# A two-layer decoder trunk on 8 cores: loads and rotary tables of the opening in another order, the first tile's attention moved into it, and steps re-ordered at the joints between tiles, before the MLP and at the final norms

## The chip, the cores and the metric

The kernel runs on all 8 cores of one Trainium2 chip, each core on its own data, without communication. The metric is the device time in microseconds (us) of the slowest core.

## The reference

```python
def reference(x, mem, positions, ...):          # x (4, 4096, 1024), mem (4, 256, 1024)
    for l in range(2):
        h = rmsnorm(x, norm_mix_g[l])
        gb, gc, xc, q, k, v = jnp.split(h @ w_in[l], splits, axis=-1)   # 512,512,512,512,128,128
        conv_out = gb * causal_short_conv(gc * xc, conv_w[l])           # depthwise, width 3
        q, k = apply_rotary(q, cos, sin), apply_rotary(k, cos, sin)
        attn_out = sliding_window_attention(q, k, v, sinks[l])          # 8 heads, 2 kv heads, window 128
        x = x + concat(rmsnorm(conv_out), rmsnorm(attn_out)) @ w_out[l]
        x = x + memory_cross_attention(rmsnorm(x), rmsnorm(mem), wx_q[l], wx_kv[l], wx_o[l])
        x = x + square(relu(rmsnorm(x) @ w_up[l])) @ w_down[l]          # 1024 -> 4096 -> 1024
    return rmsnorm(x, final_g)
```

## The kernel before

A core holds 2048 tokens and a halo of 256 before them (T = 2304), channels on partitions, f32, in SBUF all the time (`xT`). Weights come from HBM as f32 and are cast to bf16 by the transfer into a ring (`Wr`). Matmuls are bf16 with 128x128 weights.

Each layer has three stages. **p1** walks the tiles of `tiles1`. In layer 0 these are tile 0 (128 tokens, keys, values and convolution state only), tile 1 (128 tokens, the "short tile") and tiles 2 to 9 of 256 tokens; in layer 1 a halo tile and 8 full ones. For a tile: norm (`norm_a` the squares on ScalarE, `norm_r` their sum on VectorE, `norm_b` the product with ones on TensorE, a Ln and an Exp on ScalarE and eight scaled copies on VectorE, `x_h`), keys and values (`kv_a`, rotary in `kv_b`), queries (`q_a`, `q_b`), convolution (`conv_a` three projections, `conv_b` products with diagonal matrices `dg`), attention for each block of 128 (`att_s` scores, exponent and mask, `att_pv` sums and values), group norms (`g_sq`, `g_red`, `g_rest`; which 0 is convolution, 1 attention) and the output projection `p1_proj`. Iteration i works on the attention of tile i, projects tile i-1, projects queries, keys, values and convolution of tile i+1 (`nx`) and norms tile i+2 or i+3. The keys and values of the 256 memory tokens are made on the way (`mem_sq`, `mem_norm` whose scaling runs on GpSimd, `mem_piece` 0 to 7). **p2** is the cross-attention by tiles; it also norms halves of the MLP's input (`a_sq`, `a_red`, `a_rest`; the one in flight is finished by `a_pend`). **p3** is the MLP in steps (e, i) of a weight piece e and a token tile i: `up` of the next step, then `down` of this one, each output chunk `oc` added to `xT`. In the last layer it also does the final norms (`fin`), of which the second half of a tile waits in the list `rest`, and the output transfers.

All work is written out in one order by hand. Each engine runs its instructions in that order and waits on semaphores that a tracker (`Trk`) puts in front of an instruction. TensorE fills eight PSUM banks, taken in the order of least recent use. `begin` is the opening of layer 0: the rotary tables (`rope_split`, `rope_angles`, `rope_table`, `rope_spread`), the norms of tiles 0 to 3, and their keys, values and convolutions. The queue of a load is that of the engine named: `tk.dma("pool", ...)`, `load_w` and `xload` without a queue go through GpSimd's queue, in order, "sp" through SyncE's. `after("sp", ("x", 0, 16))` holds SyncE until tokens 1024 to 1279 have landed.

The order of the loads is this:

```python
tk.dma("pool", mski[:], masks_d[:], dsem("ldm"), W=["mski"])
load_kv(0); load_cv(0, 0); xload(256, 512); load_cv(0, 1); xload(512, 768)
load_q(0); load_wout(0); xload(768, 1024); xload(1024, 1280)
```

(`xload(0, 256)` stands ahead of them, on the same queue.)

## Time and profile before

| | us |
|---|---|
| median of 3 runs | 1883.87 |
| the runs | 1865.79, 1883.87, 1945.28 |
| the profiled execution, its own time | 1865.94 |
| its span on the slowest core (core 4), first to last instruction | 1864.9 |
| spans of the 8 cores | 1857.8 to 1864.9 |

The span is what the trace covers; 1.0 us of the profiled execution's own time lies around it. Granted TensorE clocks of the cores are 0.979 to 0.987 of full speed.

### The profile page before, as it was taken

The numbers are of one execution on the slowest core, as the hardware profiler recorded it, in microseconds if no ns is written. First come the engines' busy times: TensorE is split into PE (matmuls) and PEld (weight loads), VectorE is DVE, ScalarE is ACT, GpSimd is POOL, SyncE is SP. The second block draws the span as 40 slices with busy tenths as digits, with TensorE's granted clock in tenths as the row PEclk, the third lists the DMA queues.
The fourth block names the chain that finished last, engine by engine and source line by source line (L and its number), as shares of the span: only waits on it lengthen the run. The fifth ranks groups of instructions, "written<-read, shape, count | busy, mean of one in ns | idle before, by whom it ended". The sixth has DMA issues, their size and how long they took to land.

```text
span 1864.9 us, 33585 instructions; the slowest of 8 cores (1857.8 to 1864.9 us)
## 1 busy us (share of the span) xinstructions
PE 1765.1 (95%) x12355; PEld 1164.5 (62%) x12413; DVE 1185.1 (64%) x2406; ACT 704.5 (38%) x1244; POOL 71.2 (4%) x99
## 2 busy tenths in 40 slices
PE   3789998999999999999999999999999999999996
PEld 2667786888755555555557778678884444444444
DVE  4578776667575555555577878675766455455677
ACT  4445555556431111111125555564662111111232
POOL 1002000000000000000000200000000000000000
PEclk7889999999999999999999999999999999999998
DMA  9700203600332221111311011252024122200022
GB/s 183 209 1 13 35 13 61 121 2 1 61 59 41 46 46 23 24 35 34 69 24 24 13 24 24 41 97 47 1 47 86 28 46 46 40 6 1 23 68 91
DMA packets 23911, 86.38 MB, mean 46 GB/s; under 512 B 2116, under 2 KB 11332, under 8 KB 17096
## 3 DMA queue, kind: packets, MB, share of 16 engines
q0 software_dynamic: 11296, 69.47, 20.1%
q1 hardware_dynamic: 12456, 14.76, 2.4%
q8 instruction: 103, 1.69, 0.4%
q14 instruction: 56, 0.46, 0.1%
HBM read 140.06 MB, written 8.39 MB: 80 GB/s over the span
## 4 chain that ended last, share of the span: by engine, by line
PE 86%; DVE 8%; issue 3%; ACT 3%; DMA 0%; DVEq 0%; ACTq 0%; POOLq 0%
PE ps L168 85%; PE ps L180 1%; DVE S L484 1%; DVE S L760 1%; DVE xT_sb L1171 1%; DVE xT_sb L1151 1%; DVE S L474 1%; DVE S L751 1%; DVE S L627 1%; DMA xT_sb<-xT 0%; ACT S L461 0%; ACT S L463 0%; ACT S L622 0%; DVE S L641 0%; DVE H L484 0%
## 5 line engine op out<-in xcount | busy, mean ns | idle before, releaser
L168 PE MATMUL ps<-S,Wr 128*128 128x256 bf16 (+4 forms) x9494 | 1464.9, 314 | 17.9 <-DVE S L484 8.2
L168 PEld LDWEIGHTS ps<-S,Wr 128*128 128x128 bf16 x9536 | 919.2, 98 | 541.1 <-issue 34.6
L1136 ACT ACTIVATE S<-ps 128x448 bf16<-128x448 f32 (+2 forms) x292 | 162.2, 556 | 681.7 <-PE ps L168 681.7
L1151 DVE TENSOR_TENSOR xT_sb<-ps,xT_sb 128x448 f32<-128x448 f32 (+3 forms) x592 | 365.5, 631 | 57.3 <-PE ps L168 30.9
L1138 DVE TENSOR_TENSOR S<-S 128x448 bf16<-128x448 bf16 (+2 forms) x292 | 116.1, 399 | 323.7 <-ACT S L1136 323.6
L168 PE MATMUL ps<-H,Wr 128*128 128x256 bf16 (+2 forms) x1496 | 178.0, 277 | 8.2 <-DVE H L484 7.9
L168 PEld LDWEIGHTS ps<-H,Wr 128*128 128x128 bf16 x1496 | 144.6, 102 | 33.9 <-issue 15.3
L484 DVE SCALAR_TENSOR_TENSOR S<-xT_sb,cst_sb,S 128x256 bf16<-128x256 f32 (+2 forms) x360 | 140.1, 461 | 37.6 <-ACT S L463 37.6
L468 ACT ACTIVATE S<-xT_sb 128x2048 bf16<-128x2048 f32 (+3 forms) x62 | 110.8, 1788 | 9.9 <-DVE xT_sb L1151 9.9
L503 DVE TENSOR_TENSOR xT_sb<-ps,xT_sb 128x512 f32<-128x512 f32 (+1 forms) x136 | 86.1, 668 | 43.0 <-PE ps L168 42.7
L461 ACT ACTIVATE S<-ps,cst_sb 128x256 f32<-128x256 f32 (+2 forms) x97 | 45.1, 465 | 99.8 <-PE ps L168 93.6
L702 ACT ACTIVATE S<-ps 128x512 bf16<-128x512 f32 x132 | 75.0, 594 | 13.8 <-PE ps L168 7.5
L1015 DVE TENSOR_TENSOR S<-ps,S 128x512 bf16<-128x512 f32 (+1 forms) x68 | 44.6, 672 | 45.5 <-ACT S L1009 40.8
L760 DVE SCALAR_TENSOR_TENSOR S<-S,cst_sb 128x256 bf16<-128x256 f32 (+1 forms) x136 | 56.3, 476 | 26.2 <-ACT S L463 26.2
L474 DVE TENSOR_TENSOR S<-S 128x1024 bf16<-128x1024 bf16 (+2 forms) x112 | 60.2, 537 | 11.6 <-ACT S L468 5.7
L998 ACT ACTIVATE S<-ps 128x512 bf16<-128x512 f32 (+1 forms) x68 | 37.2, 573 | 61.7 <-PE ps L168 61.7
L706 DVE TENSOR_TENSOR S<-S,mski 128x1024 bf16<-128x1024 bf16 x66 | 44.9, 689 | 14.1 <-ACT S L702 13.4
L733 ACT ACTIVATE S<-S 128x512 f32<-128x512 f32 x33 | 20.8, 630 | 81.1 <-DVE S L726 75.4
L989 ACT CAST H<-ps 128x512 bf16<-128x512 f32 (+1 forms) x68 | 38.6, 569 | 31.4 <-PE ps L168 30.7
L168 PE MATMUL ps<-S,ones_d 128*128 128x256 bf16 (+2 forms) x200 | 34.4, 278 | 16.5 <-ACT S L468 16.5
L463 ACT ACTIVATE S<-S 128x256 f32<-128x256 f32 (+2 forms) x97 | 39.4, 407 | 8.9
L622 ACT COPY S<-ps 128x512 f32<-128x512 f32 (+1 forms) x34 | 19.4, 572 | 61.7 <-PE ps L168 55.4
(93 smaller groups left out, 839.3 us busy)
## 6 DMA issues: line engine op xcount, KB each, us to landing
Wr<-w_up POOLq DMA_DIRECT2D x16, 1024.0 KB, 8.6
Wr<-w_down POOLq DMA_DIRECT2D x16, 1024.0 KB, 8.7
Wr<-wx_kv POOLq DMA_DIRECT2D x16, 512.0 KB, 5.2
outT<-xT_sb SPq DMA_DIRECT2D x28, 256.0 KB, 2.5
Wr<-w_cv POOLq DMA_DIRECT2D x4, 1536.0 KB, 15.9
xT_sb<-xT POOLq DMA_DIRECT2D x5, 1024.0 KB, 35.6
Wr<-w_out POOLq DMA_DIRECT2D x4, 1024.0 KB, 27.3
xT_sb<-xT SPq DMA_DIRECT2D x2, 2048.0 KB, 16.7
```

What stands on the lines that cost most here:

```text
L168: ins = e.h.matmul(out_ap, l, r, start=(i == 0), stop=(i == n - 1))
L461: tk.op("act", lambda h: h.activation(out=dst, in_=pt[:, 0:n], func=AF.Ln, bias=col(C_EPS), scale=1.0), R=[ptok, "cst"], W=[dtok])
L468: tk.op("act", lambda h: h.activation(out=dst[:, :, 0:n], in_=xT[:, :, t0:t0 + n], func=AF.Square), R=xt(K8, t0, n), W=dtoks)
L474: tk.op("dve", lambda h: h.tensor_tensor(out=dst, in0=sq[:, 0:k, 0:n] if k > 1 else sq[:, 0, 0:n], in1=sq[:, k:2 * k, 0:n] if k > 1 else s ...
L484: tk.op("dve", lambda h: h.scalar_tensor_tensor(out=dst[:, kc, 0:n], in0=xT[:, kc, t0:t0 + n], scalar=col(gcol + kc), in1=rstd[:, 0:n], op ...
L503: tk.op("dve", lambda h: h.tensor_tensor(out=xT[:, o:o + 2, t0:t0 + n], in0=pair(pt, n), in1=xT[:, o:o + 2, t0:t0 + n], op=ALU.add), R=[pt ...
L702: tk.op("act", lambda h: h.activation(out=Eb[:, which, g, :], in_=pts[g][0][:, :], func=AF.Exp, scale=0.125), R=[pts[g][1]], W=[("E", which)])
L706: tk.op("dve", lambda h: h.tensor_tensor(out=ev, in0=ev, in1=wide(mski[:, mi * 128:(mi + 1) * 128], 8), op=ALU.mult), R=["mski"], W=[("E", ...
L760: tk.op("dve", lambda h: h.scalar_tensor_tensor(out=mixed[:, 4 * which + c, 0:n], in0=src[:, c, 0:n], scalar=col(g0 + c), in1=rstd2[:, 0:n ...
L1136: tk.op("act", lambda h: h.activation(out=o, in_=pt[:, 0:cn], func=AF.Relu), R=[ptok], W=self.hid_tok(hs, f, c0, cn))
L1138: tk.op("dve", lambda h: h.tensor_tensor(out=o, in0=o, in1=o, op=ALU.mult), W=self.hid_tok(hs, f, c0, cn))
L1151: tk.op("dve", lambda h: h.tensor_tensor(out=xT[:, oc, a:a + cn], in0=pt[:, 0:cn], in1=xT[:, oc, a:a + cn], op=ALU.add), R=[ptok], W=xt([o ...
```

## The change

The loads, the opening, iteration order in p1, the start of p2, and places in p3 are re-ordered. Tokens 0 to 255 are loaded through SyncE's queue. Queries' weights and tokens 256 to 511 go ahead of the convolution's weights. The second rotary table keeps its argument in `tmpf`, so that both sines run back to back. Tile 1's attention is in `begin`, and the loop over tiles starts at 2 in layer 0. The loads of the memory tokens and of tokens 1280 to 2303 move from SyncE's queue to GpSimd's, without the wait for tokens 1024 to 1279. The second tile of the cross-attention gets its norm in another buffer (`memn`). Removed lines begin with -, added ones with +.

```diff
...
 tk.dma("sp", sinks_b, sinks_d.partition_broadcast(128), dsem("lds"), W=[("sinks_b", 0)])
-xload(0, 256)
+xload(0, 256, "sp")
...
 load_kv(0)
+load_q(0)
+xload(256, 512)
 load_cv(0, 0)
-xload(256, 512)
 load_cv(0, 1)
 xload(512, 768)
-load_q(0)
 load_wout(0)
...
     tk.op("dve", lambda h: h.tensor_copy(out=tmpf, in_=posi), R=[RI], W=[RF])
-    tk.op("dve", lambda h: h.scalar_tensor_tensor(out=rr, in0=tmpf, scalar=-TWO_PI, in1=angf,
-                                                  op0=ALU.mult, op1=ALU.add), R=[RF, RA], W=[RR])
+    dst, dtok = ((rr, RR), (tmpf, RF))[which]
+    tk.op("dve", lambda h: h.scalar_tensor_tensor(out=dst, in0=tmpf, scalar=-TWO_PI, in1=angf,
+                                                  op0=ALU.mult, op1=ALU.add), R=[RF, RA], W=[dtok])
     if which == 0:
...
         lo, hi = -3.14159 - math.pi / 2, 3.14159 - math.pi / 2
-    tk.op("dve", lambda h: h.tensor_scalar(out=rr, in0=rr, scalar1=lo, scalar2=hi, op0=ALU.max, op1=ALU.min),
-          W=[RR])
-    if which == 0:
-        tk.op("act", lambda h: h.activation(out=tab0, in_=rr, func=AF.Sin), R=[RR], W=[("tab0", 0)])
-    else:
-        tk.op("act", lambda h: h.activation(out=tab1, in_=rr, func=AF.Sin, bias=col(C_HPI), scale=1.0),
-              R=[RR, "cst"], W=[("tab1", 0)])
+    tk.op("dve", lambda h: h.tensor_scalar(out=dst, in0=dst, scalar1=lo, scalar2=hi, op0=ALU.max, op1=ALU.min),
+          W=[dtok])
+
+def rope_sin():
+    tk.op("act", lambda h: h.activation(out=tab0, in_=rr, func=AF.Sin), R=[RR], W=[("tab0", 0)])
+    tk.op("act", lambda h: h.activation(out=tab1, in_=tmpf, func=AF.Sin, bias=col(C_HPI), scale=1.0),
+          R=[RF, "cst"], W=[("tab1", 0)])
...
-    def mem_fetch(self):
-        tk.dma("sp", memT, memT_d[:], dsem("mem"), W=[("memT", 0)])
+    def mem_fetch(self, q="sp"):
+        tk.dma(q, memT, memT_d[:], dsem("mem_" + q), W=[("memT", 0)])
         self.mem_load(0)
...
+
+        sinks_exp()
         rope_split()
         self.norm_a(0)
+        rope_angles()
+        rope_table(0)
         self.norm_b(0)
         self.norm_a(1)
-        rope_angles()
-        k0 = self.kv_a(0, 0)
-        rope_table(0)
+        rope_table(1)
         self.norm_b(1)
-        k1 = self.kv_a(1, 1)
-        rope_table(1)
-        sinks_exp()
-        self.setup()
-        self.conv_a(1, 0)
+        k = self.kv_a(0, 0)
+        rope_sin()
         rope_spread(0)
+        self.kv_b(0, *k, 0)
+        k = self.kv_a(1)
+        self.kv_b(1, *k)
+        qs = [self.q_a(1, jp) for jp in range(2)]
         self.norm_a(2)
-        self.kv_b(0, *k0, 0)
-        self.conv_b(1, 0)
-        self.norm_b(2)
-        self.kv_b(1, *k1, 1)
-        rope_spread(1)
-        k = self.kv_a(2)
-        self.conv_a(2, 0)
-        self.kv_b(2, *k)
-        rope_spread(2)
-        self.conv_a(1, 1)
-        self.norm_a(3)
-        rope_spread(3)
-        self.conv_b(1, 1)
-        self.conv_a(2, 1)
-        qs = [self.q_a(1, jp) for jp in range(2)]
         for jp in range(2):
             self.q_b(1, jp, *qs[jp])
-        after("sp", ("x", 0, 16))
-        self.mem_fetch()
-        xload(1280, 1792, "sp")
-        xload(1792, T, "sp")
+        self.att_s(1, 0)
+        self.norm_b(2)
+        self.setup()
+        self.att_pv(1, 0)
+        k = self.kv_a(2)
+        self.g_sq(1, 1)
+        self.kv_b(2, *k)
+        qs = [self.q_a(2, jp) for jp in range(2)]
+        self.g_red(1)
+        self.conv_a(1, 0)
+        for jp in range(2):
+            self.q_b(2, jp, *qs[jp])
+        self.g_rest(1, 1)
+        self.conv_b(1, 0)
+        rope_spread(1)
+        self.conv_a(2, 0)
+        self.conv_a(1, 1)
+        self.conv_b(1, 1)
+        self.norm_a(3)
+        self.g_sq(1, 0)
+        self.g_red(1)
+        rope_spread(2)
+        self.conv_a(2, 1)
+        self.g_rest(1, 0)
+        self.norm_b(3)
+        self.conv_b(2, 0)
+        rope_spread(3)
+        self.conv_b(2, 1)
+        self.mem_fetch("pool")
+        xload(1280, 1792)
+        xload(1792, T)
...
         first = NT - 8
-        for i in range(1, NT - 1):
+        for i in range(1 if self.l else 2, NT - 1):
             t0, n, ext = self.tiles1[i]
...
             nx = i + 1
-            early = self.l == 0 and i == 1
             late = self.l == 0 and i == 2
...
                 self.mem_piece(i - first - (2 if i < first + 4 else 1))
-            if i + 2 < NT and not later:
+            if i + 2 < NT and not later and not late:
                 self.norm_b(i + 2)
             self.g_sq(i, 0)
+            ahead = later or late or i == first + 1
+            if ahead:
+                self.conv_a(nx, 0)
             if i > 1 and not late:
...
                 self.mem_norm()
-            if early:
-                qs = [self.q_a(nx, jp) for jp in range(2)]
-            if later or late:
-                self.conv_a(nx, 0)
             self.att_pv(i, 0, lambda: self.g_red(i))
+            if nb > 1:
+                self.att_s(i, 1)
             if later:
                 self.norm_b(i + 2)
-            if nb > 1:
-                self.att_s(i, 1)
             if late:
                 self.p1_proj(i - 1)
-            if i > 1 and not late:
+            if i > 1 and not ahead:
                 self.conv_a(nx, 0)
...
             if i + 3 < NT:
-                self.norm_a(i + 3)
-                red = lambda: self.norm_r(i + 3)
+                ni = i + 2 if late else i + 3
+                self.norm_a(ni)
+                red = lambda: self.norm_r(ni)
             elif i + 2 == NT:
...
                 self.att_pv(i, 1, red)
+            if i != first:
+                qs = [self.q_a(nx, jp) for jp in range(2)]
+            k0 = self.kv_a(nx)
+            self.g_sq(i, 1)
             if i + 2 == NT:
                 x_rstd(self.tiles[0][1])
-            if i == first:
-                self.mem_sq()
-            if not early:
-                if i != first:
-                    qs = [self.q_a(nx, jp) for jp in range(2)]
-                k0 = self.kv_a(nx)
-            self.g_sq(i, 1)
-            if i + 2 == NT:
                 x_sq(*self.tiles[1])
...
             self.g_red(i)
-            if not early:
-                self.kv_b(nx, *k0)
-                self.conv_a(nx, 1)
-            elif red:
-                red()
+            self.kv_b(nx, *k0)
+            self.conv_a(nx, 1)
             if i + 2 == NT:
...
             self.conv_b(nx, 0)
+            self.conv_b(nx, 1)
             self.g_rest(i, 1)
-            self.conv_b(nx, 1)
+            if late:
+                self.norm_b(4)
+                self.norm_a(5)
+                self.norm_r(5)
+            if i == first:
+                self.mem_sq()
             if i + 2 == NT:
...
         self.p1_proj(i - 1, range(0, 1))
-        self.xnorm_h(0)
         pv = self.att_pv_a(i, 0)
...
         self.att_pv_c(i, 0, pv, lambda: self.g_red(i))
+        self.xnorm_h(0)
         self.mem_piece(7)
         self.p1_proj(i - 1, range(1, 2))
-        self.qproj(0, 0)
         self.att_pv(i, 1)
-        for hx in range(1, 4):
+        x_rstd(self.tiles[1][1])
+        for hx in range(4):
             self.qproj(0, hx)
-        self.xnorm_b(1)
+        self.xnorm_h(1)
         self.p1_proj(i - 1, range(2, 4))
...
         t0, n = self.tiles[i]
-        x_h(t0, n, self.cb + O_X, *HB[0])
+        x_h(t0, n, self.cb + O_X, *self.hbx(i))
+
+    @staticmethod
+    def hbx(i):
+        return (memn, [("memn", kc) for kc in K8]) if i == 1 else HB[0]
...
         c0 = (hx % 2) * 256
-        hb, HT = HB[0]
+        hb, HT = self.hbx(i)
         pt, ptok = next_ps()
...
             H = None
-            if e == 0:
-                self.a_pend()
-                if self.todo:
-                    H = self.todo.pop(0)
-                    self.a_sq(H)
+            if e == 0 and self.todo:
+                H = self.todo.pop(0)
+                self.a_sq(H)
             F = ()
...
             elif split:
-                if rest:
-                    rest.pop()()
                 self.up(*steps[si + 1], si + 1, c0=0, cn=256)
...
                 self.up(*steps[si + 1], si + 1, range(0, 2))
-                if rest:
-                    rest.pop()()
+                if e == 0:
+                    self.a_pend()
                 if H:
...
             elif not lastup:
-                self.down(e, i, si, ocs=range(4))
+                self.down(e, i, si, ocs=range(2))
                 if H:
                     self.a_rest(H)
-                self.down(e, i, si, ocs=range(4, 8))
+                if rest:
+                    rest.pop()()
+                self.down(e, i, si, ocs=range(2, 8))
             elif nxt is not None:
...
```

## Rows read from the trace of the kernel before

**Rows 1.** The page: span, share of the engines, chain that ended last by engine.

```profile
span 1864.9 us, 33585 instructions; the slowest of 8 cores (1857.8 to 1864.9 us)
...
PE 1765.1 (95%) x12355; PEld 1164.5 (62%) x12413; DVE 1185.1 (64%) x2406; ACT 704.5 (38%) x1244; POOL 71.2 (4%) x99
...
PE 86%; DVE 8%; issue 3%; ACT 3%; DMA 0%; DVEq 0%; ACTq 0%; POOLq 0%
```

**Rows 2.** Stretch of iteration 2: length, busy by engine, granted clock, DMA share, GB/s.

```profile
88.00:123.20 35.20, 29.92 (x260) 22.55 (x260) 23.11 (x51) 18.09 (x29) 0.00 (x0) 0.85 0.01 1
```

**Rows 3.** Load of the queries' weights (issued at 6.6): KB, us from issue to landing.

```profile
Wr<-w_q POOLq DMA_DIRECT2D x1, 1024.0 KB, 40.1
```

**Rows 4.** Timeline of the opening: start, duration, instruction, [idle before, releaser].

```profile
10.62 1.28 ACT L468 ACT_TABLE_LOAD   x1 [10.62 <-DMA xT_sb<-xT]
...
15.26 2.19 DVE L484 SCALAR_TENSOR_TENSOR S<-xT_sb,cst_sb,S 128x128 bf16<-128x128 f32 x8 [8.28 <-ACT S L463]
...
18.68 0.46 DVE L419 TENSOR_SCALAR Wr<-Wr 128x576 f32<-128x576 f32 x1
...
21.24 0.46 DVE L429 TENSOR_SCALAR Wr<-Wr 128x576 f32<-128x576 f32 x1
...
56.57 2.88 PE L168 MATMUL ps<-H,Wr 128*128 128x130 bf16 x48
...
88.02 1.04 PE L168 MATMUL ps<-S 64*128 64x512 bf16 x4
```

**Rows 5.** DMA queues' packets in 5-6, 15-20 and 73-76 us: packets, MB, share.

```profile
q0 software_dynamic: 47, 0.19, 75.3%
...
q0 software_dynamic: 70, 0.85, 104.7%
...
q1 hardware_dynamic: 444, 0.91, 97.5%
```

**Rows 6.** Timeline, start of iteration 3.

```profile
125.96 8.81 PE L168 MATMUL ps<-S,Wr 128*128 128x256 bf16 x64 [1.60 <-DVE S L623]
...
128.02 3.26 DVE L484 SCALAR_TENSOR_TENSOR H<-xT_sb,cst_sb,S 128x256 bf16<-128x256 f32 x8 [0.18 <-ACT S L463]
```

**Rows 7.** Timeline of TensorE: last iteration but one of both layers, and an ordinary one.

```profile
304.55 0.26 PE L168 MATMUL ps<-sqs,ones_d 128*128 128x128 bf16 x1 [3.67 <-DVE sqs L474]
...
304.61 7.40 PE L168 MATMUL ps<-H,Wr 128*128 128x256 bf16 x40
...
176.24 4.54 PE L168 MATMUL ps<-H,Wr 128*128 128x256 bf16 x40
...
1208.75 0.37 PE L168 MATMUL ps<-sqs,ones_d 128*128 128x256 bf16 x1 [4.14 <-DVE sqs L474]
```

**Rows 8.** Timeline of TensorE: iteration 2, and the same step of iteration 4.

```profile
113.47 0.37 PE L168 MATMUL ps<-S,mski 128*128 128x256 bf16 x1 [3.58 <-ACT S L676]
113.63 8.19 PE L168 MATMUL ps<-H,Wr 128*128 128x256 bf16 x48
...
182.28 5.40 PE L168 MATMUL ps<-H,Wr 128*128 128x256 bf16 x48
```

**Rows 9.** Timeline, layer 1 iteration 1, and end of an ordinary iteration.

```profile
159.13 1.67 DVE L760 SCALAR_TENSOR_TENSOR S<-S,cst_sb 128x256 bf16<-128x256 f32 x4 [0.19 <-ACT S L463]
...
1015.67 0.62 PE L180 MATMUL ps<-S,ones 128*64 128x512 bf16 x4 [2.56 <-DVE S L706]
```

**Rows 10.** Timeline, `mem_norm` beside attention in iteration 3.

```profile
136.88 4.52 POOL L778 TENSOR_TENSOR Wr<-Wr,S 128x2048 f32<-128x2048 f32 x1 [75.70 <-ACT S L463]
136.92 4.76 DVE L751 TENSOR_TENSOR S<-S 128x512 bf16<-128x512 bf16 x1
...
143.17 0.27 PE L168 MATMUL ps<-S,ones_g 128*128 128x256 bf16 x1 [0.66 <-DVE S L738]
```

**Rows 11.** Timeline, first MLP step; waits from 1450 on (us, times, longest).

```profile
511.81 0.36 PE L168 MATMUL ps<-sqs,ones_d 128*128 128x256 bf16 x1 [2.47 <-DVE sqs L474]
...
PE ps L168 <- DVE sqs L474: 7.3, 6, 4.5
```

## The prediction

> **What bounds the kernel now.** First the page: over a span of 1864.9 us TensorE is busy for 1765.1, and the chain that ended last lies on it for 86% [rows 1]. The 100 us left are all that a re-ordering of the same work can win, and besides them what a low granted clock costs: the same number of matmuls with the same columns takes longer at 1.2 GHz than at 2.4. So I listed what TensorE waits for, by stretch, and then read the timeline around each wait. Half of the idle time lies in the first 145 us, then some 4 us in each layer's last iteration but one, some 3 at the first MLP step, and 7.3 in the final norms. An ordinary iteration of p1 takes 31 us of which TensorE is busy for over 30. Iteration 2 takes 35.2 with 29.9 busy, at a mean clock of 0.85 [rows 2]. The DMA lines say that the opening is also one long transfer: the queries' weights, issued at 6.6, landed 40.1 us later, at 46.7 [rows 3].
>
> **The opening.** Before: tokens 0 to 255 had landed at 10.6, a table load of 1.28 followed, the copies of tile 0's norm ended at 15.26 + 2.19 = 17.45, and iteration 2 began with its scores at 88.0 [rows 4]. In the new order that point is the start of the loop, so the opening is worth the difference to 88.0. When the tokens land (X) is not shown, because no transfer of SyncE's queue ran beside a long backlog of GpSimd's. Alone, that queue moved 0.91 MB in 3 us [rows 5]. Bounded below: 1.05 MB at that rate from about 4 us on, and 1.5 for the end, X = 9. Above: see the first rival, X = 44. I take equal shares of the bytes, 7 us instead of 3.5, X = 12.5; it is the value nearest to the one transfer that the trace has at that place, 10.6.
>
> From X on: tile 0's norm as before without the table load, which now goes with the sinks' exponent before X, 17.45 - 10.62 - 1.28 = 5.5 us. Then VectorE makes the second table's argument, 21.24 + 0.46 - 18.68 = 3.0, and tile 1's copies, 2.2 [rows 4]: X + 10.7. Keys, values and queries of tile 1 are 48 matmuls of 128 columns, 5.8 at the low clock (twice 2.88 [rows 4]); one pair of sines with one table load runs beside them; casts and rotary steps that can't overlap I put at 2.5, an estimate: X + 19. Scores 0.6, table load 1.28, exponents and mask 3.2, Ln and Exp 0.9, copies of tile 2's norm 3.26 [rows 6]: X + 28. Keys, values and queries of tile 2 are 40 matmuls of 256 columns at the low clock, 7.4 [rows 7], and 16 of 128, 1.9: X + 37.5. What is left is TensorE's: four projections `conv_a`, two at 2.88 and two at 5.40 [rows 4, 8], and some 8 us of rotary tables, norm, rotary and diagonal products, 24.3, and 2 for waits: X + 63.8 = 76.3. The convolution's weights are there by then: all that stood before the queries' weights had landed at 46.7. **Opening: -11.7.** The memory tokens' load, the first weight piece and tokens 1280 on now stand on GpSimd's queue, where the piece waits for the last `rope_spread`, near 75, and holds the tokens behind it. They are wanted at the end of iteration 2, 30 us later, so this costs nothing; had they no such cover it would be their transfer, 14 us. The mask, keys and queries ahead of them on that queue are not hurt.
>
> **Iteration 2.** It loses the wait of 3.58 behind the memory squares, and with it the low clock: 48 matmuls took 8.19 after the wait against 5.40 in iteration 4 [rows 8]. Idle time was 5.3 [rows 2] and the low clock costs 4.2 in its two `conv_a`. I leave 2.5 for tile 3's copies, still on VectorE when `conv_a(3, 0)` wants them: **-7** (0 to -9).
>
> **Iteration 3 begins worse.** Tile 4's norm and tile 5's squares and sums are now issued at the end of iteration 2, and tile 5's norm right behind the next scores. VectorE has to do 1.67 for the attention norm [rows 9], 3.26 for tile 4 [rows 6] and 1.5 for tile 5's sums before TensorE's product for tile 5, in front of which ScalarE needs 1.9 for the start. From the last diagonal product on this is some 8.3 us, in which TensorE has 0.6 of scores to do: 7.6 idle against 1.9 now. With 2 for the clock after it and 1.6 back from the 8.81 that the projection took at a mixed clock [rows 6], **+6** (0 to +9).
>
> **`conv_a` ahead of `mem_norm`.** While GpSimd scales the memory tokens (4.52), VectorE's sum `g_red` of two bf16 tiles takes 4.76 instead of 0.5, and `g_rest` waits for it; TensorE hid this with 48 matmuls, 5.4, and waited only 0.66 [rows 10]. The change puts these matmuls before the projection. Then nothing stands between the second scores and `g_rest`: 5.4 of idle time and 1.6 of clock, once a layer. In layer 1 the matmuls fill 1.7 at the start of the iteration, where the projection waits for the norm: **+7 and +5** (0 to +8 each, if GpSimd starts when `g_red` is done).
>
> **Layer 1's iteration 1.** The mask goes ahead of tile 3's copies: most of a wait of 2.56 [rows 9], one of 1.1 behind the memory squares, and some clock. **-4** (-1 to -5).
>
> **Ordinary iterations.** `g_rest(i, 1)` goes behind the second `conv_b`, so its Ln and Exp stand behind one more copy of 0.6, and its 1.67 on VectorE, now begun at 159.13 [rows 9], end some 0.8 later. The projection that reads them starts 0.3 to 0.4 after they end now. I put 0.5 on each of ten iterations: **+5** (0 to +7).
>
> **Last iteration but one.** The sum's product waited 3.67 and 4.14, and the 40 matmuls behind it took 7.40 in layer 0 against 4.54 in an ordinary iteration [rows 7]; in layer 1 1.3 more than ordinary. It now stands behind queries, keys and values, 5.6 us of matmuls, longer than either wait. **-12** (-6 to -12).
>
> **Last tile and cross-attention.** Tile 0's copies move behind the first block's product, so the four `qproj` come 2 to 3 us before their input is there; the buffer of its own saves a wait of 0.5 to 0.7 for the second tile. **+3** (-2 to +5). **First MLP step, layer 0:** a wait of 2.47 [rows 11] and clock behind it go; the next half's norm, two chunks earlier, then may wait 2. **-3** (0 to -5). **Final norms:** six waits, 7.3, the longest 4.46 [rows 11]. The norm of a second half now stands behind 24 to 40 matmuls more, at least 5 us, which covers the three long ones, 6.4; the longest also left the clock low for some 4 us, worth 2. **-8.5** (-5 to -9). The tail behind the last matmul is the same.
>
> **Sum:** -11.7 - 7 + 6 + 7 + 5 - 4 + 5 - 12 + 3 - 3 - 8.5 = -20.2. Against the profiled execution, 1865.9, that is 1846. The median shown, 1883.9, is 18 above that execution; I forecast what a run as near the fastest would show, and a spread like that of the runs would put the median above it.
>
> **Rivals.** *The first tokens come late.* On SyncE's queue a row of tokens is a packet: 444 packets for 0.91 MB are 2 KB each, rows of 512 columns; tokens 0 to 255 have rows of 1 KB, so 1024 packets, 64 for each of 16 engines. On GpSimd's queue a packet is 12 KB of bf16 weights (70 for 0.85 MB) or 4 KB of tokens (47 for 0.19) [rows 5], 8 or 16 an engine for each load. If the engines take one packet of each queue in turn, 64 turns let through the mask, keys, queries, tokens 256 to 511, both convolution weights and half of the next tokens: all but 2 us of what had landed at 46.7 [rows 3]. X = 44 then, the loop starts at 107.8, 19.8 later than now, and the sum is +11: **1877**, slower than before. It decides from X = 24 on, where the opening gains nothing. The other re-orderings stay. For it: the sizes. Against: that the turn is a packet is seen in no row. The Trainium skill states just that turn (DMA: Bandwidth & Descriptors, section "Queues, rings and completion order": each engine goes round the queue rows and changes only at packet boundaries). By that rule X would be 44, by equal bytes 12.5; nothing else here rests on it.
>
> *The joints' gains are taken by the next wait.* Where a product is moved behind other matmuls, its Ln, Exp and copies are later too. If that costs again what the waits cost at the last iterations and half at the end, 12 us return: **1858**. Against: these results are wanted 10 us or more later. *The new idle times don't appear,* as GpSimd begins after `g_red`, and iteration 3 starts without its gap: 18 us less, **1828**. Against: nothing in the order moves the two apart. *The change does not do what it says in the opening:* TensorE waits for something else, as for tile 2's tokens, until 88: also **1858**.
>
> **From this the numbers.** Forecast 0.50 (its own range 1834 to 1856), late tokens 0.22, gains taken 0.13, no new idle times 0.10, opening unchanged 0.05. The range 1826 to 1882 takes in most of all. A change within 2%, 37 us, is what a measurement here can't tell from none: faster by more needs 1829 or less, half of the one case and a little of the forecast, 0.07; slower by more needs 1903, late tokens and every upper bound, 0.03.
>
> **What would show it.** Where the first square's activation starts (X); the first scores of iteration 2 near 76; a gap of 7 us ahead of the single 256-column product after iteration 3's first scores; a gap of 5 to 6 ahead of `g_rest` where L778 runs, in both layers; no wait at the last iteration but one; waits in the final norms under 2. The forecast is wrong if X is above 20, or if VectorE, busy for 64% overall, turns out to be late in places where I counted only TensorE.

## The result, and the profile after

The changed kernel took **1907.3 us** (median of 4 executions), the kernel before, on the same chip, 1865.8 to 1945.3. The ratio is 1.0189, with a 95% interval of 1.0119 to 1.0259. Executions in which the cores of one die ran much longer at a lower clock are left out of the ratios, here and below; milder ones of the kernel before stay in (1883.9 here, 1885.5 in runs 10 and 11) and widen the intervals, and against before's other two, 1865.8 and 1866.1, the ratio is 1.022. The change makes the kernel slower; forecast were 1846 and a range of 1826 to 1882. The span of the profiled execution is 1906.8 against 1864.9 [rows 1].

The page of the changed kernel: span, busy time, and the granted clock in tenths over 40 slices.

```profile
span 1906.8 us, 33619 instructions; the slowest of 8 cores (1893.0 to 1906.8 us)
...
PE 1769.9 (93%) x12413; PEld 1163.1 (61%) x12413; DVE 1186.6 (62%) x2406; ACT 700.4 (37%) x1242; POOL 72.2 (4%) x101
...
PE   0787999899999999999999799989999999999997
...
PEclk9888999999999999999999899999999999999999
```

TensorE is busy for 1769.9 us against 1765.1, so 37 of the 42 us more are idle time. The first slice has a 0: TensorE does almost nothing in the first 47 us. To find the rest I took the same events in both timelines, the exponents of the scores (first block of an iteration), the first exponent of each cross-attention and the last Relu, and subtracted stage by stage:

| stage | before | after | difference | forecast |
|---|---|---|---|---|
| start to first exponents of iteration 2 | 89.5 | 107.5 | +18.0 | -11.7 |
| iterations 2 and 3, layer 0 | 70.0 | 83.3 | +13.3 | +6 |
| iterations 4 to the last but one | 162.1 | 163.7 | +1.6 | -3.5 |
| last tile, layer 0 | 20.3 | 24.1 | +3.8 | +1.5 |
| cross-attention and MLP, layer 0 | 660.0 | 659.2 | -0.8 | -3 |
| iterations 1 and 2, layer 1 | 61.4 | 70.3 | +8.9 | +1 |
| iteration 3 to the last but one | 161.0 | 164.2 | +3.2 | -3.5 |
| last tile, layer 1 | 23.7 | 28.4 | +4.7 | +1.5 |
| from there to the last Relu | 596.4 | 585.8 | -10.6 | -8.5 |

The last column spreads the forecast's terms over the stages: 0.5 for each of five joints a layer and -6 for its last iteration but one make -3.5; the last tile's +3 is halved. The sum is +42.1 (the spans differ by 41.9) where -20.2 was forecast, and every stage but the last came out worse than its term. Half of the error is the first line.

The opening of the changed kernel in the timeline, with the answer to [rows 4]: start, duration, instruction, idle time before it and what ended it.

```profile
2.36 0.43 SPq L190 DMA_DIRECT2D xT_sb<-xT  x1
...
8.06 1.59 PE L168 MATMUL ps<-Wr,mski 4*128 4x288 bf16 x6 [8.06 <-DMA mski<-masks]
...
43.06 1.06 ACT L469 ACTIVATE S<-xT_sb 128x1024 bf16<-128x1024 f32 x1 [32.49 <-DMA xT_sb<-xT]
...
106.81 1.04 PE L168 MATMUL ps<-S 64*128 64x512 bf16 x4 [3.24 <-DVE S L624]
```

The 1 MB of tokens 0 to 255 is issued at 2.36 and the first square on it starts at 43.06. The loop starts at 106.81, 63.75 after X; the forecast had X + 63.8. So in this line of the table X alone was wrong: 43.1, not 12.5. The packets of the two queues in 16 to 20 us and in 25 to 30 us, in the view of [rows 5]:

```profile
q0 software_dynamic: 174, 0.80, 81.0%
q1 hardware_dynamic: 178, 0.18, 14.5%
...
q0 software_dynamic: 67, 0.82, 97.0%
q1 hardware_dynamic: 68, 0.07, 5.6%
```

As many packets of the one queue as of the other, whatever their size: when GpSimd's are 12 KB (0.82 MB in 67), SyncE's get 0.07 MB through in 5 us. That is the turn by packets that no row of before showed. The Trainium skill (DMA: Bandwidth & Descriptors, section "Queues, rings and completion order") states this turn, and the trace agrees: 67 against 68. The same load on GpSimd's queue goes in packets of 4 KB [rows 5].

At the start the turn is not one to one, and it differs by core: in 3 to 8 us SyncE's queue moved 342 packets and GpSimd's 175 on core 7, the slowest, but 507 and 171 on core 2. On cores 5, 2, 6 and 0 X is 30.1 to 35.7, on the other four 41.3 to 43.1, and the spans follow: 1893.0 to 1900.2 and 1903.2 to 1906.8. What gives a core its share at the start is not shown. The time of the kernel is that of the late cores.

TensorE's timeline at the two other places that matter, iteration 3 of layer 0, and an ordinary start with ScalarE and VectorE beside it:

```profile
148.86 0.37 PE L168 MATMUL ps<-sqs,ones_d 128*128 128x256 bf16 x1 [7.69 <-DVE sqs L475]
149.03 14.35 PE L168 MATMUL ps<-S,Wr 128*128 128x256 bf16 x112
...
171.04 0.37 PE L168 MATMUL ps<-S,ones_g 128*128 128x256 bf16 x1 [5.27 <-DVE S L752]
172.85 1.07 PE L180 MATMUL ps<-S,ones 128*64 128x512 bf16 x4 [1.44 <-DVE S L707]
```

```profile
189.49 0.58 ACT L623 COPY S<-ps 128x512 f32<-128x512 f32 x1 [0.94 <-DVE S L624]
189.59 1.91 PE L168 MATMUL ps<-S,Wr 128*128 128x256 bf16 x16 [0.25 <-DVE S L624]
...
191.06 1.67 DVE L761 SCALAR_TENSOR_TENSOR S<-S,cst_sb 128x256 bf16<-128x256 f32 x4 [0.19 <-ACT S L464]
...
192.88 1.36 PE L168 MATMUL ps<-S,Wr 128*128 128x256 bf16 x11 [1.27 <-DVE S L761]
```

The gap before tile 5's product is 7.69 (forecast 7.6), and `g_rest` waits 5.27 with 1.44 behind it (forecast 5.4), the same in layer 1 (5.24 and 1.43). In an ordinary iteration the projection now waits 1.27 for L761, the scaling at the end of the group norm. The copy of the second `conv_b` waits until VectorE has read the single buffer `y` (the view names L624, the small copy right behind that reading), and Ln, Exp and L761 stand behind this copy of ScalarE's. The waits view counts twelve of them, 15.4 us; an iteration takes 32.14 instead of 30.73.

### The profile page after: what moved, and what is told of

It reads as the page before. It is cut to its first block, busy times and chain, and to the rows that moved or that the text cites. A ratio compares the mean times of both kernels' runs of the same rounds, so it can differ in the third digit from the quotient of the medians.

```text
span 1906.8 us, 33619 instructions; the slowest of 8 cores (1893.0 to 1906.8 us)
## 1 busy us (share of the span) xinstructions
PE 1769.9 (93%) x12413; PEld 1163.1 (61%) x12413; DVE 1186.6 (62%) x2406; ACT 700.4 (37%) x1242; POOL 72.2 (4%) x101
## 4 chain that ended last, share of the span: by engine, by line
PE 87%; DVE 6%; ACT 3%; DMA 2%; issue 2%; DVEq 0%; ACTq 0%; SPq 0%
PE ps L168 85%; DMA xT_sb<-xT 2%; PE ps L180 2%; DVE S L761 1%; DVE S L485 1%; DVE S L752 1%; ACT S L462 1%; DVE S L628 1%; ACT S L623 0%; DVE S L475 0%; ACT S L464 0%; DVE xT_sb L1189 0%; DVE S L707 0%; DVE S L642 0%; DVE S L727 0%
## 5 line engine op out<-in xcount | busy, mean ns | idle before, releaser
L168 PE MATMUL ps<-S,Wr 128*128 128x256 bf16 (+4 forms) x9536 | 1468.4, 315 | 27.9 <-DVE S L761 15.4
L761 DVE SCALAR_TENSOR_TENSOR S<-S,cst_sb 128x256 bf16<-128x256 f32 (+1 forms) x136 | 56.5, 478 | 30.1 <-ACT S L464 30.1
L707 DVE TENSOR_TENSOR S<-S,mski 128x1024 bf16<-128x1024 bf16 x66 | 45.3, 693 | 26.5 <-ACT S L703 25.7
L168 PEld LDWEIGHTS ps<-S,ones_d 128*128 128x128 bf16 x200 | 19.2, 103 | 43.5 <-issue 40.6
```

The source lines that it names most:

```text
L168: ins = e.h.matmul(out_ap, l, r, start=(i == 0), stop=(i == n - 1))
L707: tk.op("dve", lambda h: h.tensor_tensor(out=ev, in0=ev, in1=wide(mski[:, mi * 128:(mi + 1) * 128], 8), op=ALU.mult), R=["mski"], W=[("E", ...
L761: tk.op("dve", lambda h: h.scalar_tensor_tensor(out=mixed[:, 4 * which + c, 0:n], in0=src[:, c, 0:n], scalar=col(g0 + c), in1=rstd2[:, 0:n ...
```

## Experiments

"Changed kernel" is the one of the diff. X is the start of the first square on tokens, the loop start that of iteration 2's first scores. Runs 2 to 8 are single executions, runs 1, 9, 10 and 11 several.

One stretch differs between the cores of one execution: iterations 2 and 3 of layer 0 take 67.1 to 68.0 on four cores of the kernel before and 69.8 to 70.0 on the other four, in the changed kernel 80.7 to 81.2 on three and 83.1 to 83.6 on five. In the changed kernel it is mostly the clock: 48 matmuls ahead of iteration 3's scores take 5.40 on the three cores of the lower level and 7.07 on four of the five others. The table has the slowest core, which is of the higher level in both kernels. A difference of 2.6 in this stretch can thus be the level alone.

### 1 to 3. Where do the 30 us of the tokens come from?

Early tokens in the changed kernel:

```diff
-        xload(0, 256, "sp")
+        xload(0, 256)
```

> The changed kernel with one word undone: tokens 0 to 255 are again the first transfer of the GpSimd queue, ahead of masks and weights; all else of the change stays. Theory A (the late tokens are what made the opening late, and the rest of the new opening is good for what the prediction gave it): the first square starts near 10.6 us as before instead of 43.1, the first scores of iteration 2 near 10.6 + 63.8 = 74.4 instead of 106.8, and the whole is some 32 us shorter than the changed kernel, near 1875 us, the same as the kernel before within 1%. Theory B (the new opening is itself longer than the old, or it is then held up by tokens 256 to 511 or by the query weights, which now land later in the chain's time): the scores of iteration 2 start at 85 or later and the whole is at 1885 or more. Ordinary iterations stay at 32.1 us under both.

The kernel before with the opposite edit (`xload(0, 256)` becomes `xload(0, 256, "sp")`):

> The kernel before with one word changed: tokens 0 to 255 go to the SyncE queue behind positions and sinks; everything else is as before. If the two queues are served packet for packet in turn while both have work, the 1 MB of small packets lands only with the 5 to 7 MB of weights beside it, and the first square starts near 41 us (30 us later than before's 10.6); the scores of iteration 2, at 88.0 before, move by about as much, to 115 or 120. If instead bytes, not packets, were shared evenly, 1 MB would be there after 2 MB in all, near 12 us, and nothing would move. If the late tokens of the changed kernel came of something else in it (the order of its weights), the square starts under 20.

The changed kernel with the GpSimd queue re-ordered, tokens 0 to 255 still on SyncE:

```diff
-        load_kv(0)
-        load_q(0)
         xload(256, 512)
-        load_cv(0, 0)
-        load_cv(0, 1)
         xload(512, 768)
-        load_wout(0)
         xload(768, 1024)
         xload(1024, 1280)
+        load_kv(0)
+        load_q(0)
+        load_cv(0, 0)
+        load_cv(0, 1)
+        load_wout(0)
```

> The changed kernel with tokens 0 to 255 still on the SyncE queue, but the GpSimd queue ordered so that its own small packets lie beside them: tokens 256 to 1279 first, then keys and values, queries, convolution, output weights. Turn by turn between queues, small packet against small packet, the 1 MB on SyncE needs only about 2 MB in all before it is there: first square near 12 to 20 us. If the SyncE queue is simply served last or thinly whatever the other queue holds, the first square is no earlier than the 43.1 of the changed kernel. The weights of keys and values then land after 4 MB more, so the loop starts near 95 or 100 in either case; the time of the whole is not the question here.

Measured, from the timelines of the three in this order:

```profile
10.46 1.06 ACT L469 ACTIVATE S<-xT_sb 128x1024 bf16<-128x1024 f32 x1 [3.58 <-DMA xT_sb<-xT]
11.88 1.59 PE L168 MATMUL ps<-Wr,mski 4*128 4x288 bf16 x6 [11.88 <-DMA mski<-masks]
...
78.31 1.04 PE L168 MATMUL ps<-S 64*128 64x512 bf16 x4 [3.24 <-DVE S L624]
```

```profile
38.77 1.28 ACT L468 ACT_TABLE_LOAD   x1 [38.77 <-DMA xT_sb<-xT]
40.07 1.06 ACT L468 ACTIVATE S<-xT_sb 128x1024 bf16<-128x1024 f32 x1
```

```profile
17.02 1.06 ACT L469 ACTIVATE S<-xT_sb 128x1024 bf16<-128x1024 f32 x1 [6.24 <-DMA xT_sb<-xT]
...
87.27 1.04 PE L168 MATMUL ps<-S 64*128 64x512 bf16 x4 [3.24 <-DVE S L624]
```

Run 1 took 1881.0 us, ratio to before 1.008 (1.0056 to 1.0105), 26.3 below the changed kernel. Run 2 took 1893.2, 26.7 above before: one word, and every later stage shifted by 27.2 to 27.7. In run 3 X fell from 43.1 to 17.0 though the tokens stayed on SyncE, because the packets beside them were 4 KB ones of tokens instead of weights. So it is the size of the neighbour's packets times one's own count of 1024, not the queue's standing, and not the rest of the change. (Over the cores X is 35.8 to 40.1 in run 2, 16.6 to 18.5 in run 3 and 9.5 to 10.8 in run 1.) Here too the turn is not one to one at the start: in 4 to 8 us SyncE's queue moved 639 packets and GpSimd's 139. Why is not shown.

Run 1 also shows what the prediction had missed in the good case: with early tokens the loop starts 67.9 behind X, not 63.8. The mask, behind 1 MB of tokens on its queue, lands at 11.88, and the rotary angles that begin with it are no longer ready when tile 0's norm is: its copies on VectorE stand behind them and begin 6.7 behind X instead of 3.3. The loop starts 9.7 earlier than before (88.0 [rows 4]); and still the kernel is 15 us slower than before. The rest of the loss lies in the joints.

### 4 and 5. The ordinary iterations

A second buffer for `y` (`gcs`, free at that point, takes the second pair):

```diff
-                    tk.op("act", lambda h: h.copy(out=ybuf[:, :, 0:n], in_=pair(py, n)), R=[pyt], W=[("y", 0)])
+                    yb, ytok = ((ybuf, ("y", 0)), (gcs, ("gcs", 0)))[cp]
+                    tk.op("act", lambda h: h.copy(out=yb[:, :, 0:n], in_=pair(py, n)), R=[pyt], W=[ytok])
...
```

> The changed kernel with a second buffer for the convolution's output: the second pair of channels goes through the gate's buffer (gcs), free by then, instead of through y, so its copy by ScalarE need not wait for the first pair's product on VectorE. Theory A: that wait (0.94 us on the copy at L623, with conv_b 0 and 1 now back to back) is what pushes logarithm, exponent and the mixing later, so the wait of 1.27 to 1.37 us on L761 falls to 0.4 or less in each ordinary iteration, and an iteration goes from 32.1 to about 31.3; 10 such, 8 to 10 us in all. Theory B: the wait on L761 comes from the attention's normalising chain behind the second conv_b on TensorE and ScalarE whatever the buffer; it stays over 1.0 and the total within 3 us of the changed kernel's 1907.

The old order of the joint:

```diff
                     self.conv_b(nx, 0)
-                    self.conv_b(nx, 1)
                     self.g_rest(i, 1)
+                    self.conv_b(nx, 1)
```

> The changed kernel with one pair put back everywhere in the attention loop: first pair's diagonal product, then the attention group's norm, then the second pair's diagonal product, as before; late tokens and all else stay. Theory A (the joint's order alone makes each ordinary iteration longer: the scores' exponents and the mixing stand behind the second pair's copy): the iteration goes from 32.1 back to 30.7 or 30.8 us, the wait on L761 from 1.3 to 0.3 or less, and the whole is 13 to 15 us shorter, near 1893. Theory B (what makes the iterations longer is more than this pair, since the second y buffer alone took off 0.7 of the 1.4): the iteration stays at 31.3 or more and the whole at 1898 or more.

The same spot of the ordinary iteration shown above, with two buffers, and then the joint in the old order one iteration on:

```profile
185.75 0.59 ACT L624 COPY S<-ps 128x512 f32<-128x512 f32 x1 [0.24 <-PE ps L168]
...
189.14 5.07 PE L168 MATMUL ps<-S,Wr 128*128 128x256 bf16 x45 [0.57 <-DVE S L762]
```

```profile
213.28 0.82 PE L168 MATMUL ps<-S,dg 128*128 128x256 bf16 x6
213.94 0.27 PE L168 MATMUL ps<-S,ones_g 128*128 128x256 bf16 x1
214.47 0.82 PE L168 MATMUL ps<-S,dg 128*128 128x256 bf16 x6 [0.25 <-DVE S L624]
215.22 0.60 PE L168 MATMUL ps<-S 64*128 64x512 bf16 x4
215.84 1.91 PE L168 MATMUL ps<-S,Wr 128*128 128x256 bf16 x16
217.58 0.27 PE L168 MATMUL ps<-sqs,ones_d 128*128 128x256 bf16 x1
217.69 4.53 PE L168 MATMUL ps<-S,Wr 128*128 128x256 bf16 x40
```

With two buffers the wait fell from 1.27 to 0.57 and an iteration from 32.14 to 31.45; total 1894.5, 12.8 less where 8 to 10 were expected. With the old order the wait on L761 is gone, an iteration takes 30.73 as before, and the kernel 1886.2: 21 less where 13 to 15 were expected. The joint also stands in the iterations around `mem_norm`: layer 1's first two are 1.9 shorter. Iterations 2 and 3 of layer 0 are 3.8 shorter, but that run's slowest core is of the lower level; at equal level they are 1.2 shorter (80.7 to 79.5). And X came 2 earlier in that execution. So the joint is worth 17 to 20 us in all, by core. In an ordinary iteration the single buffer is half of the loss (0.70 of 1.41); the other half is the place of the norm behind the second product.

### 6 to 8. The 5.3 us in front of `g_rest`

```diff
-                    ahead = later or late or i == first + 1
+                    ahead = later or late
```

> The changed kernel with one place put back: in the second iteration of layer 1 (and only there, since layer 0's second also is 'late' by another name) the first projection of the convolution follows the output projection and the memory norm instead of going ahead of them. The wait of 5.24 us on L752 and of 1.43 on L707 behind it, which stand between the attention product and the norm of the convolution's half, go to 0 to 0.5 in layer 1 and stay in layer 0; the waits of the old order (the memory norm's 0.66 to 2.56) come back. Net 4 to 6 us less from layer 1's third iteration on, near 1902; a rival, that the wait is on the memory norm's own chain on GpSimd and VectorE wherever the projection stands, would leave 5 us there and the time where it is.

(The text on record names the place wrongly: `i == first + 1` is iteration 3 in layer 0 and iteration 2 in layer 1, so the edit acts in both layers, and the 5 us were to go in both.)

```diff
-                    if i == first + 1:
-                        self.mem_norm()
                     self.att_pv(i, 0, lambda: self.g_red(i))
+                    if i == first + 1:
+                        self.mem_norm()
```

> The changed kernel with the memory norm behind the attention product of the first block instead of ahead of it, in both layers; the projection stays ahead. Theory A (VectorE's queue has the group reduction of L752 behind the memory norm's part, whose reciprocal root waits for GpSimd's work or for ScalarE, so L752 comes 5 us late): the waits of 5.24 and 5.27 on L752 and of 1.43 behind each go to under 0.7, together 10 to 13 us less, near 1895; GpSimd's scaling of the memory tokens starts some 5 us later and its first piece of keys is still in time. Theory B (the first piece of memory keys waits for the later scaling): what is gained comes back as a wait before the first mem_piece of the fourth iteration, and the iteration after starts no earlier.

The scaling of the memory tokens (L779) on VectorE (`"pool"` becomes `"dve"` in its one line):

> The changed kernel with one instruction on another engine: the multiplication of the memory tokens by their root (128 x 2048 fp32, L779, 4.50 us on GpSimd) runs on VectorE; the eight scalings behind it stay on GpSimd, and the order of TensorE's and ScalarE's work is the changed kernel's. Theory A (a VectorE instruction on bf16 tiles of the on-chip memory that meets L779 is held until L779 ends: L752 took 5.26 for two instead of 0.81 in the changed kernel, and with the memory norm behind it L752 took 0.81 and the mask L707 behind it 4.52): L752 takes 0.8 for two again although the eight scalings still run beside what follows; the wait in front of the group product falls from 5.27 by the difference between 4.5 and the multiplication's own time on VectorE, which by the four times 512 fp32 elements at 0.69 each is near 2.8 at most, so to 1 to 3.5 us, in both layers; 4 to 8 us less in all. Theory B (any work of GpSimd's holds VectorE): the eight scalings, 0.65 each, hold L752 or L739 and L707 in turn, and the wait stays at 4 us or more.

The same stretch in the changed kernel (first), with the projection back, with the norm later, and with L779 on VectorE:

```profile
165.48 4.50 POOL L779 TENSOR_TENSOR Wr<-Wr,S 128x2048 f32<-128x2048 f32 x1 [59.79 <-ACT S L464]
165.52 5.26 DVE L752 TENSOR_TENSOR S<-S 128x512 bf16<-128x512 bf16 x2
```

```profile
158.81 5.41 PE L168 MATMUL ps<-S,Wr 128*128 128x256 bf16 x48
158.98 4.93 DVE L752 TENSOR_TENSOR S<-S 128x512 bf16<-128x512 bf16 x2
...
164.65 0.27 PE L168 MATMUL ps<-S,ones_g 128*128 128x256 bf16 x1 [0.43 <-DVE S L739]
```

```profile
163.04 0.81 DVE L752 TENSOR_TENSOR S<-S 128x512 bf16<-128x512 bf16 x2
...
165.59 4.50 POOL L779 TENSOR_TENSOR Wr<-Wr,S 128x2048 f32<-128x2048 f32 x1 [61.60 <-ACT S L464]
166.72 4.52 DVE L707 TENSOR_TENSOR S<-S,mski 128x1024 bf16<-128x1024 bf16 x2 [1.28 <-ACT S L703]
...
171.39 1.06 PE L180 MATMUL ps<-S,ones 128*64 128x512 bf16 x4 [6.94 <-DVE S L707]
```

```profile
163.87 2.29 DVE L779 TENSOR_TENSOR Wr<-Wr,S 128x2048 f32<-128x2048 f32 x1 [1.26 <-ACT S L464]
...
166.68 0.81 DVE L752 TENSOR_TENSOR S<-S 128x512 bf16<-128x512 bf16 x2
...
167.63 0.29 PE L168 MATMUL ps<-S,ones_g 128*128 128x256 bf16 x1 [3.42 <-DVE S L752]
...
171.50 1.06 PE L180 MATMUL ps<-S,ones 128*64 128x512 bf16 x4 [3.57 <-DVE S L707]
```

With the projection back (1896.0 us, 11.3 less, of which some 2 are an earlier X) L752 is still held, 4.93 for its two, but 48 matmuls cover it: the waits are 0.43 and 1.05. Iterations 2 and 3 of layer 0 are 7.0 shorter and layer 1's first two 3.3. With the norm later (1906.5) nothing is gained: now `g_red` takes 0.81, but the mask product, the next VectorE instruction with both inputs in on-chip bf16 tiles, takes 4.52 until L779 is done, and TensorE waits 6.94 for it. With L779 on VectorE (1905.4, where 4 to 8 us less were expected) nothing is held and the theory of the hold is right, but its gain is not there: 3.42 and 3.57 are 7.0 us of waiting, as 5.27 and 1.44 were 6.7. (Its slowest core has 80.8 for iterations 2 and 3, as the changed kernel has on cores of that level, and 70.3 for layer 1's first two, as there.) Without 48 matmuls to do, TensorE meets the chain of multiplication, sum, Ln, Exp, exponents and masks whatever holds it. The cover was what mattered, not the hold. Where GpSimd's piece of the work should stand is second to that.

### 9. The gains alone

The kernel before, with the reciprocal root of the last iteration but one moved behind keys and values, and the MLP loop of the changed kernel:

```diff
                     self.g_sq(i, 1)
                     if i + 2 == NT:
+                        x_rstd(self.tiles[0][1])
                         x_sq(*self.tiles[1])
...
```

> The kernel before with two of the change's parts alone: the reciprocal root of the cross-attention's norm later in the last iteration but one of each layer, and the new order of halves and norms in the MLP with its final norms. Theory A, from the two traces: each late root takes off 5 to 6 of the 6 us that it stands for (3.67 and 4.14 there, with 1.0 coming back) and the MLP and final norms take off 10 in all, together 14 to 20 us, so 1846 to 1852 from 1866. Rival: the MLP's gain seen in the changed trace came only with its new last tile of the attention; then the two are worth 6 to 8 us and the time is 1858 to 1860, within 2% of before in either case.

TensorE's waits for sums (L474 is the line of [rows 11]) over the whole execution, and the last iteration but one:

```profile
PE ps L168 <- DVE sqs L474: 3.7, 4, 2.8
```

```profile
306.58 5.40 PE L168 MATMUL ps<-H,Wr 128*128 128x256 bf16 x48 [0.95 <-ACT S L461]
```

1846.3 us, ratio 0.9894 (0.9874 to 0.9914): 19.3 less than before. Waits on the sums fall from 17.6 to 3.7. The last iteration but one is 5.4 shorter in layer 0 and 4.4 in layer 1 (0.95 comes back as a wait for the second half's squares), and from layer 1's first cross-attention exponent to the last Relu it is 10.8. The rival, that the MLP gains only with the new last tile, fell.

### 10 and 11. The mended kernel

The changed kernel with early tokens (1), the old joint (5) and the projection back (6), and tile 5's norm later:

```diff
-                    if i + 2 < NT and not later and not late:
+                    third = self.l == 0 and i == 3
+                    if i + 2 < NT and not later and not late and not third:
                         self.norm_b(i + 2)
...
-                    if later:
+                    if later or third:
                         self.norm_b(i + 2)
```

> The changed kernel with four mends together: tokens 0 to 255 first on the GpSimd queue, the old order of the two diagonal products around the group norm, the projection of the third iteration of layer 0 and the second of layer 1 back behind the output projection, and in layer 0's third iteration the norm of tile 5 behind the second block's scores instead of ahead of tile 2's output projection. Its opening, last iteration but one, last tile, MLP and final norms are the changed kernel's. Worked out from the stages seen so far, against the kernel before: scores of iteration 2 9.7 us earlier (as in the run with early tokens), first scores of iteration 4 some 13 earlier (the 7.7 idle before tile 5's product gone, if theory A holds that only its place in the order made it), ordinary iterations at 30.7, last iteration but one 5 to 6 earlier in each layer, last tile 4 later in each, MLP and final norms 10 earlier: near 1841. If the 7.7 us come back as a wait further on in that iteration (the product of tile 5 is late wherever it stands), 1848. If the separate mends don't add up, over 1855.

The same with the last tile of before, and in layer 1's iteration 1 `norm_b` ahead of `att_s(i, 1)`:

> The same mended kernel with the last tile of the attention also in the old order (halves and output projection between the query projections as before, one half buffer, root and copies of the second half together), and in layer 1's first iteration the norm ahead of the second block's scores as before. Theory: from the first scores of the last tile to the first exponent of the cross-attention 20.2 us again instead of 24.1, in both layers, and layer 1's first iteration 1 us shorter; 8 to 9 us less than the other mended kernel, near 1832 and 1.8% faster than before. Rival: the old last tile lets the cross-attention start sooner, but its own first step or the first MLP step, which need the second half's queries and the norms, then wait as long; the two mended kernels are within 3 us of each other.

In the first one, iteration 3 of layer 0:

```profile
120.74 1.03 PE L168 MATMUL ps<-S,ones_d 128*128 128x256 bf16 x8 [0.76 <-ACT S L703]
123.40 0.62 PE L180 MATMUL ps<-S,ones 128*64 128x512 bf16 x4 [1.63 <-DVE S L707]
...
125.97 6.73 PE L168 MATMUL ps<-S,Wr 128*128 128x256 bf16 x48
...
141.64 7.07 PE L168 MATMUL ps<-S,Wr 128*128 128x256 bf16 x48
```

It took 1846.5 us where 1841 were expected; the ratio is 0.9863 (0.972 to 1.0006). The 7.7 us in front of tile 5's product are gone, and yet iterations 2 and 3 take 72.4, where run 6, with the gap, has 76.4. By the cores of the lower level the other mends leave 72.9 (80.7 in the changed kernel, 79.5 in run 5, 74.1 in run 6), by the higher 75.0 (83.5, 82.2, 76.3); all cores of run 10 have 72.1 to 72.5. So moving the norm gave 0.6 to 2.7 of the 7.7, some 2 in the mean over the cores: waits of 0.4 to 1.6 stand further on, 5.7 in all ahead of iteration 4, and 48 matmuls take 6.73 and 7.07 where run 6, with the gap, has 5.41 and 5.40. The rival of the text on record, that the 7.7 come back further on (1848), held in the main.

The second took **1838.4 us**, ratio 0.9818 (0.9722 to 0.9915), 8.2 less than the first, as expected (8 to 9), though 6 above the 1832 expected, since the first stood 6 above its own. Its last tiles take 20.3 and 23.7 as before, the first one's 22.5 and 28.6. It is the best of all: 27 us faster than the kernel before and 69 faster than the changed one.

## Why the prediction was wrong, step by step

- **The tokens (X), the step that failed.** The bounds held, 9 and 44, and so did the packets' sizes and the turn in the rival, which had a chance of 0.22: X 44 and loop start 107.8 forecast there, 43.1 and 106.8 measured. That this agrees to 1 us holds for the late cores alone; on the other four X is 30.1 to 35.7. I took 12.5, the value "nearest to the one transfer that the trace has at that place", but that transfer stood on the other queue, in other packets. Equal bytes had no row for them either. Runs 1 to 3 show the cost: 26 to 27 us in the total. With X = 43.1 in place of 12.5 the sum would have been +10, still 32 short of the +42 measured.
- **From X to the loop.** 63.8 forecast, 63.75 measured, and this was partly luck. With the early tokens that the forecast stood on it is 67.9: I hadn't followed the mask through its own queue, and only late tokens gave it the time. On the way, too, errors cancelled: tile 2's queries were done at X + 35.3 (forecast 37.5), and the rest took 28.5 (26.3).
- **Iteration 2, -7, and layer 1's iteration 1, -4: mis-sized.** From scores to scores iteration 2 got 2.0 shorter (35.2 to 33.2). In place of waits of 1.12 and 3.58 it has 0.90 and 2.21, the latter for attention's last product on VectorE, and the clock that I gave back whole stayed low: the two groups of 48 matmuls take 7.49 and 7.07 instead of 6.78 and 8.19. Layer 1's iteration 1 got 1.2 longer: the wait of 2.56 fell to 0.27, but 2.48 and 1.93 stand ahead of later products, and the 48 matmuls behind them take 7.07 instead of 5.40. Swapping norm and scores back made layer 1's first two iterations 2.6 shorter (runs 10 and 11).
- **Iteration 3's start, +6.** The gap was as forecast, 7.69 against 7.6. Its removal gave some 2 of the 7.7 (run 10): a gap can be priced rightly and yet not be won back by moving it.
- **`conv_a` ahead, +7 and +5.** Place and length right: 5.27 and 5.24, 1.4 behind each; undone, 7.0 and 3.3. The reason given, that matmuls that hid the hold went away, is what runs 6 to 8 showed.
- **Ordinary iterations, +0.5 each: mis-sized.** Measured +1.41 each. I had counted one more copy in front of Ln and Exp and left out that this copy waits for the single `y`. Over the loops that is 9 us of error; with the same joint in the iterations around `mem_norm`, run 5 gives back 17 to 20 (21 on the slowest core, with 1.6 of X and 2.6 of the clock's level in it).
- **Last iteration but one, -12.** -5.4 and -4.4 by run 9, whose joint is the old one; about 1 came back in each layer.
- **Last tile, +3: mis-sized.** +3.8 and +4.7. Run 11 takes 2.2 and 4.9 off it; in run 10 the first one was down to 22.5 already.
- **MLP and final norms, -3 and -8.5.** Layer 0 gave 0.1 (run 9), as the first MLP step still waits 2.76 for the next half's sums; the final part gave 10.8.

Nearly all of these errors have one sign. Each piece was priced by the wait that it removes and by the one wait that I saw coming, and in the tight stretches VectorE and ScalarE made two or three small ones more. The text on record named this as a sign of being wrong, VectorE late in places where only TensorE was counted, and the other sign as well, X above 20. Not settled: why layer 1's first two iterations are 1.3 longer in run 9 than before, with their order unchanged (before has 61.4 on six of its cores, 61.5 and 62.7 on the others; run 9 62.4 to 62.7 on seven and 61.0 on one).

## What to carry to other kernels

Before a load moves to another queue, count its packets there: beside a backlog nearly every one can wait for one of the other queue's. From issue to first use 1024 packets of 1 KB took 28 to 41 us by core beside weights, 14 to 16 beside 4 KB packets, and the same load from the head of the other queue, as 4 KB packets, 8 to 9. Compare stages on more than the slowest core: here one and the same stretch differed by 2.6 us between cores of one execution. A re-ordering is as good as what remains to cover the chain of the other engines: look at which matmuls stand between a result's last input and its first reader, and at every single buffer on the way. And undo the parts of a mixed change one by one: here two parts held 19 us of gain, beneath 61 us of loss.

## What was unexpected in the hardware

That `g_red` is slow beside GpSimd stood in [rows 10]. Not expected was that the hold passes to whatever comes next: with the norm later, `g_red` took 0.81 and L707 4.52 for two, until L779's 4.50 were over. L727, which has an input in a ps tile, took 0.69 in run 10 in the middle of L779. The Trainium skill (SBUF — State Buffer, section "Who interferes with whom") says that a VectorE instruction with two inputs in the on-chip memory contends with one of GpSimd's that reads it, one with at most one such input, outside its two-port modes, doesn't, and the second to start waits for the first to end; the trace agrees with 4.52, 5.26 and 0.69. By the same rule each of the eight scalings behind L779, some 1.0 long and reading on-chip memory too, should hold such an instruction that starts inside it. There the measurement differs: in run 8 L752 takes 0.81 for two and L707 0.69 each, all inside these scalings. So not all of GpSimd's work holds VectorE, and what sets the two kinds apart is not shown.

The second thing is the clock. The windows of iteration 3, of run 6 with the gap and of run 10 without: stretch, length, busy by engine, granted clock (1.00 is 2.4 GHz), DMA share, GB/s.

```profile
147.00:158.00 11.00, 10.86 (x81) 8.43 (x81) 7.01 (x14) 6.28 (x9) 0.00 (x0) 0.80 0.00 1
158.00:180.00 22.00, 20.39 (x186) 16.19 (x185) 19.30 (x31) 12.10 (x20) 12.68 (x9) 1.00 0.00 1
```

```profile
110.00:125.00 15.00, 10.92 (x93) 8.12 (x91) 10.64 (x24) 9.80 (x15) 0.57 (x1) 1.00 0.01 1
125.00:149.00 24.00, 22.23 (x172) 17.00 (x173) 21.72 (x38) 11.68 (x20) 12.53 (x9) 0.86 0.01 2
```

With the gap the clock is low right behind it and full from 158 on; without the gap it is full at first and falls to 0.86 in the mean after a stretch with 4 us idle in pieces. Counted in matmuls, run 6 loses 2.0 behind the gap (64 take 9.17, at full clock 7.15) and run 10 3.0 (6.73 and 7.07 for 48 each, at full clock 5.40). The low clock was not avoided, only moved on, and with it part of the gain.
